# Three row slots tile by tile at six block boundaries, a third head slot, one borrowed weight buffer, and a merged up projection

## What is computed

```python
for l in range(2):                                     # first model, two layers
    x = x + 0.5 * rmsnorm(swiglu(rmsnorm(x), w_in, w_out))          # D_FF = 2816
    x = x + rmsnorm(hybrid_mixer(rmsnorm(x)))          # 14336 + ... columns of projections
    x = x + 0.5 * rmsnorm(swiglu(rmsnorm(x), w_in, w_out))
u = rmsnorm(x)                                         # second model, one layer
h = x + rmsnorm(attention(u) @ w_o)
a = relu(rmsnorm(h) @ w_up)                            # 1024 -> 4096
h = h + rmsnorm((a * a) @ w_down)
out = h + rmsnorm(sigmoid(h @ w_gate + b) * (p @ w_proj))
```

## Time and profile before

| | |
|---|---|
| three runs | 2034.25, 2031.1, 2032.05 us; median 2032.05 |
| profiled execution | 2034.39 us, of which the span is 2032.2 |
| TensorE busy | 1994.3 us (98%), 11612 matmuls |
| VectorE, ScalarE, GpSimd busy | 1299.5, 983.2, 102.9 us (64%, 48%, 5%) |
| DMA queue with the weights | 352.34 MB, 52.7% of 16 engines' span; a 1 MB slot lands 4.9 to 5.5 us after issue |
| largest groups | wide slots L1534 and L1535 451.1 and 359.2 us (1280 each), column slots L1522 to L1524 306.5, 303.3, 303.3 us (1072 each), row slots L1741, L1551 |

### The profile page before, as it was taken

The page is one execution under the profiler, slowest core; times in us unless marked ns, Lnnn a source line. Parts: engine busy times, 40 slices in busy tenths (PEclk is TensorE's granted clock), DMA queues, the critical chain, the costliest instruction groups (busy, mean ns, idle before and its releaser), DMA issues.

```text
span 2032.2 us, 27980 instructions
## 1 busy us (share of the span) xinstructions
PE 1994.3 (98%) x11612; PEld 1748.8 (86%) x11612; DVE 1299.5 (64%) x1601; ACT 983.2 (48%) x1358; POOL 102.9 (5%) x211
## 2 busy tenths in 40 slices
PE   9999999999999999999999999999999999999996
PEld 7888998879898888888889987888888888889985
DVE  7656777546556674766569754465667566766555
ACT  5445465354434544544455644543454445754443
POOL 1003000000000000100300000000010001010000
PEclk9999999999999999999999999999999999999999
DMA  7656456535656556565554464455655656345661
GB/s 252 203 186 212 131 187 202 192 125 167 205 188 207 166 187 201 172 206 187 191 193 165 150 224 149 163 186 187 207 168 187 228 184 194 119 156 188 186 208 61
DMA packets 245148, 369.31 MB, mean 182 GB/s; under 512 B 6679, under 2 KB 180023, under 8 KB 245022
## 3 DMA queue, kind: packets, MB, share of 16 engines
q1 hardware_dynamic: 240000, 352.34, 52.7%
q0 software_dynamic: 4528, 14.85, 2.2%
q10 hardware_dynamic: 494, 0.32, 0.1%
HBM read 366.28 MB, written 1.08 MB: 181 GB/s over the span
## 4 chain that ended last, share of the span: by engine, by line
PE 89%; DVE 5%; ACT 2%; DMA 1%; issue 1%; POOL 1%; DVEq 0%; SPq 0%; POOLq 0%; ACTq 0%
PE ps L1741 19%; PE ps L1551 19%; PE ps L1534 14%; PE ps L1535 7%; PE ps L1522 6%; PE ps L1524 6%; PE ps L1523 6%; PE ps L1612 4%; PE ps L1576 1%; DMA raw<-in_ffn_w_in_dram 1%; DVE w_lo L1016 1%; PE ps L1685 1%; DVE u L1066 1%; DVE a L1171 1%; PE ps L1896 1%
## 5 line engine op out<-in xcount | busy, mean ns | idle before, releaser
L1016 DVE TENSOR_TENSOR w_lo<-raw,w_hi 128x1024 fp32r<-128x1024 f32 (+1 forms) x658 | 765.5, 1207 | 366.5 <-ACT w_hi L658 364.7
L658 ACT ACTIVATE w_hi<-raw 128x1024 fp32r<-128x1024 f32 (+1 forms) x658 | 653.1, 1042 | 392.3 <-PE ps L1551 196.1
L1534 PE MATMUL ps<-u,w_hi 128*128 128x512 f32 x1280 | 451.1, 397 | 0.3 <-DVE act L1125 0.3
L1535 PE MATMUL ps<-u,w_lo 128*128 128x256 f32 x1280 | 359.2, 281 | 0.0
L1522 PE MATMUL ps<-u,w_hi 128*128 128x256 f32 x1072 | 306.5, 286 | 0.1
L1524 PE MATMUL ps<-u,w_lo 128*128 128x256 f32 x1072 | 303.3, 283 | 0.0
L1523 PE MATMUL ps<-u,w_hi 128*128 128x256 f32 x1072 | 303.3, 283 | 0.0
L1534 PEld LDWEIGHTS ps<-u,w_hi 128*128 128x128 f32 x1280 | 240.2, 188 | 59.0 <-issue 0.8
L1535 PEld LDWEIGHTS ps<-u,w_lo 128*128 128x128 f32 x1280 | 241.8, 189 | 0.2
L1741 PE MATMUL ps<-w_hi,u 128*128 128x512 f32 x640 | 205.4, 396 | 2.0 <-DVE w_lo L1016 2.0
L1522 PEld LDWEIGHTS ps<-u,w_hi 128*128 128x128 f32 x1072 | 205.6, 192 | 1.4 <-issue 0.8
(11 more groups left out here) (279 smaller groups left out, 2517.0 us busy)
## 6 DMA issues: line engine op xcount, KB each, us to landing
raw<-in_w_mix_in_dram SPq DMA_DIRECT2D x112, 1024.0 KB, 5.1
raw<-in_ffn_w_in_dram SPq DMA_DIRECT2D x88, 1024.0 KB, 5.1
raw<-in_ffn_w_out_dram SPq DMA_DIRECT2D x40, 1024.0 KB, 4.9
raw<-in_w_ret_out_dram SPq DMA_DIRECT2D x16, 1024.0 KB, 5.0
raw<-in_w_up_dram SPq DMA_DIRECT2D x16, 1024.0 KB, 5.5
raw<-in_w_down_dram SPq DMA_DIRECT2D x16, 1024.0 KB, 4.9
raw<-in_w_in_dram SPq DMA_DIRECT2D x9, 1024.0 KB, 5.3
raw<-in_w_lru_out_dram SPq DMA_DIRECT2D x8, 1024.0 KB, 5.0
```

The costliest lines, as they stand in the source:

```text
L658: A(parts(n)[0][:, part], raw[i % RAW][:, part], ACT.Copy).then_inc(heads_done, 1)
L1016: V.tensor_tensor(parts(n)[1][:, part], raw[i % RAW][:, part], parts(n)[0][:, part], ALU.subtract)\
L1534: M(ps[:, bank0 + a, :], hi[:, k, c], u[:, :, k, :], start=k == 0, stop=False)
L1535: ins = M(ps[:, bank0 + a, 0:S], lo[:, k, c], u_hi[:, k, :], start=False, stop=k == KD - 1)
```

## The change

- `FFN_SLOTS` loses one slot: pair 8's two half slots become one row slot.
- The entry slot of the six blocks after the first (`LENT`) is split into `lent_hi`/`lent_lo`, which share the memory of a3 and a0. It isn't in the ring, nor split by `due`, but by `EARLY` during the row phase of a feed-forward (slot r = 4) or the mixer's ret_out.
- `long_rows` replaces the last row slots at g = 1 to 6: three slots on tile 0, three on tile 1, with `turn(g, 0)` ahead of the last half bank. ScalarE and VectorE have a `long_boundary` with a new order.
- At g = 1 to 5 (`THREE_HEADS`) slot 2 of the block is a head slot too: `enter` runs three on tile 0, with the second turn inside the third, and three on tile 1; `turn_back` has three slots of transposes, to banks 4, 5 and 6. In a feed-forward this is pair 1's gate (`plain_gate`); TensorE then runs pair 1's up slot and turns back after it. In the mixer `turn_back` stands after slot xa 3.
- The 14 column slots of the up projection become wide slots; ScalarE copies the low half, VectorE adds the halves, and one operation does Relu and square.
- At the last layer, GpSimd's loads of the bias constants wait for the head slots (slot_used).

```diff
-FFN_SLOTS = FFN_OUT2 + LAST_PAIRS + 1
+FFN_SLOTS = FFN_OUT2 + LAST_PAIRS
...
+THREE_ROWS, THREE_HEADS = range(1, G_UP), range(1, G_UP - 1)
 HEADSLOT = {}
 for _g, _c in enumerate(ENTRY):
-    HEADSLOT[_c], HEADSLOT[_c + 1] = (_g, 0), (_g, 1)
+    for _i in range(3 if _g in THREE_HEADS else 2):
+        HEADSLOT[_c + _i] = (_g, _i)
 ASIDE = {_c + 1: _g for _g, _c in enumerate(ENTRY)}
+LENT = {ENTRY[_g] for _g in THREE_ROWS}
...
+        EARLY[_base + 2 * FIRST_PAIRS + 4] = _base + FFN_SLOTS
         EARLY[_base + FFN_OUT2 - 4] = _base + FFN_SLOTS + 1
+    EARLY[_l * SLOTS + AT["ret_out"] + 5] = _l * SLOTS + FFN2
...
-    return n + 2 if n not in HEADSLOT and n - 1 not in ASIDE and n + 2 < B_END and n + 2 not in ASIDE else None
+    if n in HEADSLOT or n - 1 in ASIDE or n - 1 in HEADSLOT and HEADSLOT[n - 1][1] == 2:
+        return None
+    return n + 2 if n + 2 < B_END and n + 2 not in ASIDE and n + 2 not in LENT else None
...
-        if n + 1 in HEADSLOT and n + 1 not in ASIDE:
+        if n + 1 in ENTRY:
             order += [m for m in (n + 3, n + 4, n + 5) if m < B_END]
+            if n + 3 in HEADSLOT:
+                order.append(n + 6)
...
-        a0 = sb("a0", [P, 8 * (S + 3)])
-        a1, a2, a3, a4, a5 = (sb(f"a{i}", [P, 2048]) for i in range(1, 6))
+        with ExitStack() as shared:
+            a0 = shared.enter_context(nc.sbuf_tensor("a0", [P, 8 * (S + 3)], F32))
+            a3 = shared.enter_context(nc.sbuf_tensor("a3", [P, 2048], F32))
+        lent_lo = sb("lent_lo", [P, 8 * (S + 3)], F32R)
+        lent_hi = sb("lent_hi", [P, 2048], F32R)
+        a1, a2, a4, a5 = (sb(f"a{i}", [P, 2048]) for i in (1, 2, 4, 5))
...
+        def plain_gate(l, which, p):
+
+            return p == 0 or p == 1 and 3 * l + 2 * which in THREE_HEADS
...
+                    until(slot_used, ENTRY[3 * l + 2] + 3)
...
+            def long_boundary(g, by):
+                n = ENTRY[g]
+                post_square(g, 0, by)
+                post_square(g, 1, by)
+                pre_squares(g, 0)
+                head(n + 2)
+                post_square(g, 2, by)
+                u_heads(g, 0)
+                post_square(g, 3, by)
+                pre_squares(g, 1)
+                head(n + 3)
+                u_heads(g, 1)
+                head_copy(g, 0)
+                head(n + 4)
+                if g in THREE_HEADS:
+                    third_copy(g, 0)
+                head_copy(g, 1)
+                if g in THREE_HEADS:
+                    third_copy(g, 1)
+                    head(n + 5)
...
+                    if plain_gate(l, which, p):
+                        act.sem_inc(gate_low.sem, 1)
+                    else:
+                        silu_of_sum(l, which, p)
                     if p > 0:
-                        silu_of_sum(l, which, p)
                         up_lows(l, which, base, p)
                     else:
-                        act.sem_inc(gate_low.sem, 1)
...
-                        A(act2[:, p % 2, :], ps[:, (9 + p) % 4, :], ACT.Relu).then_inc(b["relu_ready"], 1)
+                        if p < 2:
+                            A(act2[:, p % 2, :], ps[:, 4 + p, :], ACT.Copy).then_inc(b["relu_low"], 1)
+                        else:
+                            A(act2[:, p % 2, :].rearrange("p (a n) -> p a n", a=2), wide_halves(2 * (p % 2))[1], ACT.Copy)\
+                             .then_inc(b["relu_low"], 1)
...
+            def long_boundary(g):
+                n = ENTRY[g]
+                dve.wait_ge(gain_loaded.sem, gain_loaded.at(g, 16))
+                gain_half(g, 0)
+                gain_half(g, 1)
+                add(g, 0)
+                add(g, 1)
+                dve.wait_ge(pre_gain_loaded.sem, pre_gain_loaded.at(g, 16))
+                pre_gains(g, 0)
+                pre_scales(g, 0)
+                rest(n + 2, 0)
+                u_rests(g, 0)
+                gain_half(g, 2)
+                gain_half(g, 3)
+                add(g, 2)
+                add(g, 3)
+                pre_gains(g, 1)
+                rest(n + 2, 1)
+                pre_scales(g, 1)
+                u_rests(g, 1)
+                rest(n + 3)
+                rest(n + 4)
+                if g in THREE_HEADS:
+                    rest(n + 5)
...
-                if p > 0:
+                if not plain_gate(l, which, p):
...
-                own.done(V.memset(xa_pad[:, :, 0:3], 0.0))
                 for name, count in STAGES:
                     for j in range(count):
                         n = l * SLOTS + AT[name] + j
@@ -1227,6 +1309,9 @@
                         if (name, j) in (("sc_out", 3), ("mix_out", 1)):
                             mix_rests(l, 0 if name == "sc_out" else 1)
                         ahead(n)
+                        if (name, j) == ("xa", 2):
+                            emptied(n)
+                            own.done(V.memset(xa_pad[:, :, 0:3], 0.0))
...
-                        dve.wait_ge(b["relu_ready"], p + 1)
-                        V.tensor_tensor(mul2[:, p % 2, :], act2[:, p % 2, :], act2[:, p % 2, :], ALU.mult)\
-                         .then_inc(b["sq_ready"], 1)
+                        dve.wait_ge(b["relu_low"], p + 1)
+                        if p < 2:
+                            dve.sem_inc(b["relu_summed"], 1)
+                        else:
+                            low = act2[:, p % 2, :].rearrange("p (a n) -> p a n", a=2)
+                            V.tensor_tensor(low, wide_halves(2 * (p % 2))[0], low, ALU.add).then_inc(b["relu_summed"], 1)
+                            dve.wait_ge(b["relu_summed"], p + 1)
+                        V.scalar_tensor_tensor(mul2[:, p % 2, :], act2[:, p % 2, :], 0.0, act2[:, p % 2, :], ALU.max,
+                                               ALU.mult).then_inc(b["sq_ready"], 1)
...
+            def long_rows(g, n, k0, act_hi, act_lo, waits):
+
+                for tt in range(TT):
+                    for i in range(2):
+                        if waits[i] is not None:
+                            pe.wait_ge(*waits[i][tt])
+                        ins = row_part(n + i, (k0 + 2 * i, k0 + 2 * i + 1), act_hi, act_lo, (tt,), False, False, 4)
+                        if tt == 1:
+                            ins.then_inc(slot_used, 1)
+                    if waits[2] is not None:
+                        pe.wait_ge(*waits[2][tt])
+                    tok = slice(P * tt, P * tt + P)
+                    hi, lo = row_view(n + 2)
+                    for half in range(2):
+                        for k in range(2):
+                            if tt == 0 and half == 0:
+                                split_part(n + 2, k)
+                            for a, (stat, mov) in enumerate(((act_hi, hi), (act_hi, lo), (act_lo, hi))):
+                                ins = M(ps[:, 4 + 2 * tt + half, :], stat[:, k0 + 4 + k, tok],
+                                        mov[:, k, 512 * half:512 * half + 512], start=False, stop=k == 1 and a == 2)
+                        ins.then_inc(slot_used if tt == 1 and half == 1 else rows_done.sem, 1)
+                        if tt == 1 and half == 0:
+                            turn(g, 0)
...
             def enter(g):
 
-                turn(g, 0)
+                if g not in THREE_ROWS:
+                    turn(g, 0)
                 head_slot(g, 0, 0)
-                head_slot(g, 1, 0, turn_next=True).then_inc(head_mm.sem, 1)
-                for i in range(2):
+                if g in THREE_HEADS:
+                    head_slot(g, 1, 0).then_inc(head_mm.sem, 1)
+                    head_slot(g, 2, 0, turn_at=4).then_inc(head_mm.sem, 1)
+                else:
+                    head_slot(g, 1, 0, turn_at=6).then_inc(head_mm.sem, 2)
+                for i in range(3 if g in THREE_HEADS else 2):
...
             def turn_back(g, banks):
 
+                for tt in range(TT):
+                    pe.wait_ge(head_rows.sem, head_rows.at(g, 2 * tt + 2))
                 for i, bk in enumerate(banks):
                     for tt in range(TT):
-                        if i == 0:
-                            pe.wait_ge(head_rows.sem, head_rows.at(g, tt + 1))
+                        rows = mul2[:, tt, S * i:S * i + S] if i < 2 else third_rows(tt)
                         for a in range(2):
                             o = S * a + P * tt
-                            ins = nc.tensor.transpose(ps[:, bk, o:o + P], mul2[:, tt, S * i + P * a:S * i + P * a + P],
-                                                      ident[:, :])
+                            ins = nc.tensor.transpose(ps[:, bk, o:o + P], rows[:, P * a:P * a + P], ident[:, :])
                 ins.then_inc(head_turned.sem, 1)
...
-                wide_slot(n, 0)
-                if p == 1:
+                    wide_slot(n, 0)
+                    pe.wait_ge(mul_ready.sem, mul_ready.at(l, pair))
+                    wide_slot(n + 1, 2)
+                elif plain_gate(l, which, p):
+                    wide_slot(n + 1, 2)
```

(35 more changed lines are left out.)

71 lines of the change are left out of this document (40 added, 31 removed).

## The result

| | before | after |
|---|---|---|
| median of six runs each, same chip | 2032.58 us (2031.1 to 2034.25) | 2040.87 us (2038.39 to 2044.52) |
| ratio, 95% interval | | 1.0039 (1.0028 to 1.0050) |
| profiled execution, its span | 2034.39, 2032.2 | 2044.52, 2042.7 |
| mean granted clock of the profiled execution | 0.998 | 0.994 |

The changed kernel is 8.3 us slower (5.7 to 10.2 by the interval); 3.5 was forecast. The six executions of the changed kernel differ by 6 us, and their mean granted clocks go with it: 2038.39 and 2039.25 us at 0.997, 2040.07 and 2041.88 at 0.995, 2041.67 and 2044.52 at 0.994. A difference of 0.003 in the mean clock of a 2040 us program stands for 6.1 us.

The account below looks back on a forecast made before the run. TensorE's own work and pauses were taken to bound the kernel. Won 13.35 and lost 16.9 us made it 3.5 slower: 2037.9 for the profiled execution, median 2035.5, range 2028 to 2042.

Parts of the forecast that it names:

- rival (c): Boundaries g = 1 to 5: late ScalarE split delays the third square, first pause returns; 5.8 us more, 2041.3; chance 0.13.
- rival (d): Mixer's wait before q 3: clock falls to 1.2 GHz for one column slot, 5.8 us, twice; 2047; chance 0.10.
- What bounds the kernel: Whole kernel: TensorE is busy 98% of 2032.2 us, so only its own work and its pauses can move the end.
- Part 1: Boundaries, three row slots tile by tile with first turn inside: 11.3 us won at g = 1 to 5, 0.65 at g = 6.
- Part 2: Borrowed buffer, entry slot's split and load moved into row phase and ret_out: costed at 0; uncovered, one slot costs 2.3 us.
- Part 3: Third head slot at five boundaries and its turning back: 0.65 us lost by slots, 2.2 us by added transposes.
- Part 4: Up projection, 14 column slots become wide: 1.4 us won, VectorE's added operation hidden.
- Part 5: Feed-forward at g = 2, 3, 5: new TensorE wait for pair 1's gate signal, 2.35 us each, 7.05 us lost.
- Rival (a): Feed-forward: gate signal leaves early with pair 0's first multiply, each wait 1.2 us; 3.5 us less, 2032.0; chance 0.13.
- Part 6: Mixer at g = 1, 4: new TensorE wait before q 3 for VectorE's weight split, 3.5 us each, 7.0 us lost.
- Rival (b): Mixer: q 3's split comes in time and the wait is covered; 7.0 us less, 2028.5; chance 0.12.
- The sum of waits and work: Whole kernel: 13.35 us won, 16.9 us lost, net 3.5 us slower.

Follow-up runs that it names:

- e6: Changed kernel with two head slots at every boundary, third head and its place for turning back taken out: 2035.31 us, 1.0010 of the kernel before.
- e5: Kernel before with only the merged up projection (14 column slots made wide): 2032.37 us, 0.9985 of the kernel before.
- e4b: Changed kernel with 9 and 14 dummy matmuls filling TensorE's waits after turning back and before q 3: 2035.67 us, 1.0008 of the kernel before.
- e0: Changed kernel unchanged, run again on the chip of e3, e4b and e8: 2041.08 us, 1.0036 of the kernel before.
- e1: Changed kernel with VectorE's signal for pair 1's gate sent with pair 0's at g = 2, 3, 5: 2034.03 us, 0.9994 of the kernel before.
- e2: Changed kernel with the split of q 3's weights, and the next one, made one slot earlier in the mixer: 2033.18 us, 0.9991 of the kernel before.
- e3: Changed kernel with the edits of e1 and e2 together: 2025.27 us, 0.9954 of the kernel before.
- e4: Changed kernel with 18 and 29 dummy matmuls in TensorE's waits after turning back and before q 3, outlasting them: 2049.74 us, 1.0071 of the kernel before.
- e8: e3 with VectorE's second half split of slot +2 moved behind tile 1's scaling: 2025.63 us, 0.9960 of the kernel before.

## Why the prediction was right in its waits and short in the time

The median was forecast at 2035.5 and came at 2040.87; the profiled execution at 2037.9 and came at 2044.52. The measured median lies inside the stated range of 2028 to 2042, and that is luck: the range reached so far up for rival (c), 2041.3, which did not happen, and it left out rival (d), the clock, which is what made the difference. The 8.3 us are also twice the 4.1 within which the prediction put its largest share. (The shares were added up wrongly: two fifths of 0.52, 0.13 and 0.10 give 0.44 for slower, not 0.42.) Step by step:

- **What bounds the kernel**: right. What changed the time were TensorE's pauses, its own work and its clock.
- **Part 1, g = 1 to 5**: right. 0.1 is left of the 2.4 at each, where 0.15 was forecast. **g = 6**: the second turn waits 2.06 where 1.1 was forecast. The term that was mis-sized is GpSimd's: it was taken from a place where VectorE did something else, and the half split beside it makes the first of its two operations 1.46 long instead of 0.40. The same slow operation stands at g = 1 (210.25), where the third head hides it. It costs 1 us, once: with the 0.5 behind the second turn, which stayed, g = 6 now loses 2.7 where 2.4 to 2.5 was lost before, so nothing is won there.
- **Part 2**: no weight split and no load appears as a releaser inside the boundaries; 0 stands as far as the rows can tell.
- **Part 3**: not measured by itself in a run. By the rows at g = 1, 60 head matmuls lie between 205.80 and 213.04, so a head slot is 5.79 where 5.83 was taken, and about 0.5 is lost instead of 0.65. e6 shows what the third head is worth: without it the second turn waits some 2.1 at six boundaries instead of one.
- **Part 4**: right as far as e5 can tell, 1.5 by spans and 2.5 (1.2 to 4.9) by medians against 1.4, and no wait.
- **Part 5**: right in kind and size, 2.18 against 2.35, three times. The increment left at the start of VectorE's operation, not at its end. The Trainium skill (PSUM — Partial Sum Buffer, "Engine vs sequencer instructions") says the sequencer waits for dispatch and not for completion; the trace agrees, with 883.02 against 882.93. Rival (a), the increment running past its engine's queued waits, did not happen.
- **Part 6**: right in kind. From the gates to q 3 it is 4.19 in after and 1.07 in the kernel before (251.57 to 252.64): 3.1 lost against 3.5, twice. Rival (b) falls by the same rows.
- **Rival (c)**: did not happen; ScalarE's third square was in time.
- **The sum of waits and work**: 3.5 was forecast. The terms as measured are 11.5 won at g = 1 to 5 and 1.5 in the up projection, and lost 0.2 at g = 6, 2.7 by the third head and its transposes (the latter as forecast), 6.5 and 6.2 by the two kinds of wait: net 2.6. With the clock held up (e4b) it is 1.5 by medians (-0.2 to +3.7) and 1.7 by spans. So the sum was right in kind and 1 to 2 us too high; parts 5 and 6, taken too long, and g = 6, taken too good, cancel in part.
- **Rival (d), the clock**: this is the step that fell short. It was put at nothing in the sum and given a tenth, only for the two longest pauses, at 5.8 each. In fact a stretch at 1.2 GHz came with each of the six pauses of 3.3 us in the profiles of after, e0 and e1, and with ten of the 22 pauses of 2.03 to 2.18 us in all profiles of kernels that have them (after 1 of 4, e0 2 of 4, e1 0 of 1, e2 2 of 4, e3 1 of 1, e4 1 of 1, e4b 0 of 1, e6 3 of 6). It costs about 1.5 where it lasts 3.4 us and 2.5 where it lasts 6.8 and begins inside the pause, less than (d)'s price but at more places: 5.5 in the profiled execution, and 5.4 by the medians of e0 and e4b. I had kept it as an exception because the longest pause before, apart from the first load, was 1.8 with the clock up. That row says nothing of longer pauses, and a clock term belonged on all five new ones. The Trainium skill (TensorE: Matmul & The Clock Gate, "What's actually happening") had the lower level follow idleness of this order, and the trace agrees, with 0.50 behind a pause of 3.33. By its rule the pauses of 2.03 to 2.18 would be too short; ten of them were not, and there the measurement decides. I cited it and did not let it into the sum.

By the spans, 10.5 between the two profiled executions: about 1.7 waits and moved work (e4b), 0.9 the first load, 5.5 the clock, and 2.1 that the kernel before had won by a faster pace of some wide slots (last section), which is not the change's doing; 0.3 is left over. What stays open: which of the pauses of 2.2 us costs the clock in a given execution. Of the three profiles that have those after turning back (after, e0, e2), g = 3 lost it in all, g = 2 in one and g = 5 in one. All pauses of 2.03 to 2.18 stand next to transposes, twelve ahead of them at turning back or eight behind them in the second turn, and those of 3.3 do not; whether transposes count as work for the clock, no run tests.

## What to carry to other kernels

In a kernel in which TensorE is busy 98% of the time, a new pause is to be priced twice: by its length, and, from about 2 us on, by a stretch at half the clock (here 1.5 us, at times 2.5), with a chance that grows with the pause: here none in 1.8 us or less, ten in 22 at 2.0 to 2.2, six in six at 3.3. When a step such as turning back is moved later, list every signal that was given behind it on the other engines: both kinds of pause came from a signal and a split that did not need the moved work and only stood in line behind it, and moving these two turned 1.0036 into 0.9954. An engine's duration read at one place holds only while its neighbours do the same work beside it (here 0.40 against 1.46). And two profiled executions can differ by 1 to 2 us for a reason that is not the change: compare medians of the same chip, or stage with stage.

## What the runs showed of the hardware that was not expected

- The granted clock falls behind pauses of 2.06 and 2.18 us (e3, after), not only behind 3.3; in another execution of the same program it can stay up behind the same pause. Column matmuls then follow at 0.213 instead of 0.120, in the profile of e1:

```profile
254.42 0.41 PE L1613 MATMUL ps<-u,w_hi 128*128 128x256 f32 x1
254.63 0.41 PE L1614 MATMUL ps<-u,w_hi 128*128 128x256 f32 x1
```

- A GpSimd operation on one column of 128 partitions takes 0.40 alone and 1.46 while VectorE's 1.22 us subtraction of two SBUF operands runs beside it; over the whole kernel the 32 operations of that line average 569 ns in e3 and 365 in e8:

```profile
L527 POOL TENSOR_SCALAR small<-small 128x1 f32<-128x1 f32 x32 | 18.2, 569 | 981.5 <-ACT a L692 940.9 <-ACT a L701 40.6
```

```profile
L527 POOL TENSOR_SCALAR small<-small 128x1 f32<-128x1 f32 x32 | 11.7, 365 | 983.1 <-ACT a L692 942.5 <-ACT a L701 40.6
```

  The Trainium skill (SBUF — State Buffer, "Who interferes with whom") says that a VectorE instruction with two SBUF inputs contends with a GpSimd instruction that reads SBUF; these rows agree.
- The filler's passes over the identity follow each other at 0.11 to 0.12 (58 in 6.64 us, 28 in 3.29), but the profile shows two of them for each matmul of the program (58 for 29, 28 for 14), so one costs 0.23, twice a transpose of the same size (0.109).
- The wide slots run at one of two paces with the clock up throughout, and which one changes from one execution of a program to the next. From turning back at g = 2 to the first turn at g = 3 it is 163.84 us in after and 162.58 in e0, the same kernel, with a granted clock of 1.00 all through the wide slots of both:

```profile
689.64 1.03 PE L1752 MATMUL ps<-ident,mul 128*128 128x128 f32 x8
853.48 0.71 PE L1709 MATMUL ps<-ident,a 128*128 128x128 f32 x5
```

```profile
688.29 0.93 PE L1752 MATMUL ps<-ident,mul 128*128 128x128 f32 x7
850.87 1.03 PE L1709 MATMUL ps<-ident,a 128*128 128x128 f32 x8
```

  In that stage's wide slots ahead of the row slots the mean distance from one 512 column matmul to the next is 0.353 us in after and 0.347 in e0. The pace holds for a whole stage of slots or a long part of one. The profile of the kernel before has the faster pace at g = 2 and in part at g = 5, which is worth 2.1 us (221 pairs at 0.006, 219 at half of that); e4b has it only in a part of the up projection, 0.5, and after nowhere. What decides it is open.
